# Two-layer hybrid decoder trunk: norm weights spread by one-column products, rank sums in one pass, the experts' order ahead of the gates, the first expert unit in halves

## The chip, the cores and the metric

The kernel runs on one NeuronCore of a Trainium2 chip. The metric is the device time of one execution in microseconds (us).

## The reference

The input is x, 256 tokens of 1024 channels, float32. Two layers run one after the other. Each has a mixer part (three groups of heads that read one RMS-normed input: a convolution, an SSD scan and latent attention, with one output projection behind them) and a channel mixer. In layer 1 the channel mixer sends each token to two of eight experts:

```
h = h + concatenate([y_conv, y_ssd, y_mla]) @ w_out[i]
hn = rms_norm(h, ffn_norm_g[i])                 # the norm weights g_ffn of the text
logits = hn @ router                            # 256 x 8
top_val, top_idx = top_k(logits, 2)
gates = softmax(top_val)
y[token] += gate * ((silu(hn @ wg[e]) * (hn @ wu[e])) @ wd[e])   # for both experts e of a token
h = h + y;  h = h + (p[i] @ ple_w_proj[i]) * sigmoid(rms_norm(h, g) @ ple_w_gate[i])
```

Each expert has three matrices of 1024 x 3584 (wd 3584 x 1024). Layer 0 has one dense SwiGLU in place of the experts. A last RMS norm ends the trunk.

## The kernel before

Nothing schedules the kernel but its own text: each engine's program is written out by hand, in `block.tensor`, `block.scalar`, `block.vector`, `block.sync` and `block.gpsimd`, and engines wait for each other on semaphores. Each engine works through its list in order.

**Weights.** All large weights come in units of 128 partitions x 2048 float32 (1 MB). SyncE issues the transfers into `ring`, which has 7 slots (`SLOTS`); unit g goes to slot g mod 7, once TensorE has read the unit seven before it. A unit is then parted in two, so that products can be made in fp32r: ScalarE copies it to `w_hi` (`split`, L1354, in the expert part `moe_split`, L1360), six of which exist, and VectorE writes what is left to `ring_lo` (L1856, L1862). TensorE waits for `lo_ready` of the unit and makes three products for each tile: high by high, high by low, low by high (`product`, L556 to L558).

**Mixers' end, layer 1.** VectorE adds up the scan's parts and multiplies them with the gate z (L2106, `ygz_ready`). ScalarE squares the result (L1531), takes roots (L1535) and squares the conv part (L1537, `csq`); VectorE makes reciprocals (L2121), scales, and writes the rests of the transposed heads (L1868, L1869). TensorE transposes (L814), makes the variance of the conv part (L823) and then runs four output units, pair 3 first, into four PSUM banks. VectorE adds the sums to h (L2154) and writes xs = h * g_ffn (L2158), for which the 1024 norm weights must stand in every partition, in `gain_of`. They lie one to a partition at the start. The kernel makes them so: ScalarE scales the identity by each of eight columns (`gain_diag_f`, L1522), TensorE multiplies by a square of ones (L804), and ScalarE copies out of PSUM (L1526).

**Routing.** TensorE makes the logits (L942). VectorE takes the two largest of each token (L2195 to L2219) and writes 0/1 rows, `counted`. TensorE sums them in three float32 products (L947 to L949): by a triangle for a token's rank within its expert, by ones for the experts' counts. VectorE makes the gates from ScalarE's exponential (L1615, L2224 to L2229), puts them with the ranks, the experts' numbers and the counts in a `table` of six vectors of eight, and sorts all six by count (L2245 to L2253). From the sorted table come the number of pairs and the experts' order (`order`, L2256 to L2262, `flag_ready`), then the slots of the tokens and the first selection matrix (`build_sel`, L2280).

**Experts.** SyncE waits for `flag_ready`, loads an expert's number into a register and issues its units (28 units of wg and wu, 14 of wd; 336 in all for eight experts). An expert pair has a heavy one (up to 128 tokens a step) and a light one (64). TensorE gathers tokens by products with the selection matrix (`gather`, L964); ScalarE and VectorE take them out as high part and rest, first half of the channels ahead of unit 0 and second half behind unit 1 (`take_heavy`). Unit c of the heavy expert (`in_unit`) has 12 products of 512 columns. On ScalarE and VectorE the parting runs four units ahead (`MOE_LEAD`), with the gate's silu (L1637) in ScalarE's list ahead of unit 7.

## Time and profile before

| | |
|---|---|
| median of 3 runs | 1526.2 us (1523.24 to 1528.65) |
| profiled execution, its own time | 1526.69 us |
| its span, first to last instruction | 1524.9 us |
| TensorE busy | 1458.8 us (96%) |
| VectorE busy | 1211.4 us (79%) |
| ScalarE busy | 1025.2 us (67%) |
| HBM traffic | 289 GB/s over the span |

The span is from one profiled execution; what lies around it is 1.8 us. Matmuls are pipelined: a row's length is longer than the distance to the next, and the distance is what a product costs. A float32 product leaves two records, an fp32r product one.

### The profile page before, as it was taken

The page shows a single profiled execution, that of the slowest core. Times are in us where ns is not written, and L with a number is a line of the kernel's source. Part 1 is how long each engine was busy: PE and PEld are TensorE (multiplying, and loading weights), DVE is VectorE, ACT ScalarE, POOL GpSimd, SP SyncE. Part 2 cuts the span into 40 slices and gives each one's busy share as a digit, 9 for nine tenths or more (in the row PEclk, how much of TensorE's full clock was granted, in tenths as well). Part 3 has the DMA queues.
Part 4 walks back from the last instruction along what each step waited for, and adds up shares of the span by engine and source line. Part 5 has one row for each costly group of instructions (what it writes and reads, how often), then busy time and mean ns, then how long its engine had stood idle before and what let it go on. Part 6 is the DMA issues. An engine that isn't in the chain of part 4 may idle for free.

```text
span 1524.9 us, 18697 instructions
## 1 busy us (share of the span) xinstructions
PE 1458.8 (96%) x7062; PEld 1199.6 (79%) x7062; DVE 1211.4 (79%) x1122; ACT 1025.2 (67%) x960; POOL 5.6 (0%) x12
## 2 busy tenths in 40 slices
PE   6989999999899879999999999999999999999997
PEld 5867888888797668878888887887877887887766
DVE  4996544653579769899999999999889999889973
ACT  5565443441655648778878788877788877788854
POOL 0000000000000000000000000000000000000000
PEclk9999999999999989999999999999999999999999
DMA  9414555555440049999999999999999999999980
GB/s 301 155 67 145 185 190 194 180 185 193 151 159 36 0 165 409 344 393 409 399 387 405 363 410 408 390 398 381 352 410 407 383 398 379 347 410 406 369 300 28
DMA packets 143865, 441.83 MB, mean 290 GB/s; under 512 B 6928, under 2 KB 21552, under 8 KB 143776
## 3 DMA queue, kind: packets, MB, share of 16 engines
q1 hardware_dynamic: 143104, 438.51, 76.8%
q0 software_dynamic: 672, 2.13, 0.4%
q8 instruction: 57, 0.93, 0.2%
q14 instruction: 32, 0.26, 0.0%
HBM read 439.56 MB, written 1.05 MB: 289 GB/s over the span
## 4 chain that ended last, share of the span: by engine, by line
PE 80%; DMA 9%; DVE 6%; ACT 3%; issue 1%; SPq 0%; DVEq 0%; ACTq 0%
PE psum L556 17%; PE psum L558 17%; PE psum L557 17%; DMA ring<-in_moe_w_down 5%; PE psum L1022 4%; PE psum L1023 4%; PE psum L1045 3%; PE psum L1046 3%; PE psum L1075 3%; PE psum L604 3%; DMA ring<-in_moe_w_up 3%; DVE ring_lo L1862 2%; PE psum L971 2%; PE psum L964 2%; ACT w_hi L1360 2%; PE psum L577 1%
## 5 line engine op out<-in xcount | busy, mean ns | idle before, releaser
L1862 DVE TENSOR_TENSOR ring_lo<-ring,w_hi 128x2048 fp32r<-128x2048 f32 x337 | 764.8, 2288 | 82.0 <-ACT w_hi L1360 79.5
L1360 ACT ACTIVATE w_hi<-ring 128x2048 fp32r<-128x2048 f32 x337 | 643.0, 1917 | 147.0 <-DMA ring<-in_moe_w_up 53.6
L1856 DVE TENSOR_TENSOR ring_lo<-ring,w_hi 128x2048 fp32r<-128x2048 f32 (+1 forms) x69 | 155.0, 2266 | 112.4 <-ACT w_hi L1354 112.4
L558 PE MATMUL psum<-w_hi,hidden_b 128*128 128x512 f32 x560 | 219.3, 392 | 0.0
L556 PE MATMUL psum<-w_hi,hidden_b 128*128 128x512 f32 x448 | 180.0, 402 | 3.7 <-DVE ring_lo L1856 3.7
L1022 PE MATMUL psum<-w_hi,xT_parts 128*128 128x512 f32 x448 | 180.0, 402 | 1.0 <-DVE ring_lo L1862 0.7
L557 PE MATMUL psum<-ring_lo,hidden_b 128*128 128x512 f32 x448 | 175.1, 391 | 0.0
L1023 PE MATMUL psum<-ring_lo,xT_parts 128*128 128x512 f32 x448 | 174.9, 391 | 0.0
L556 PE MATMUL psum<-w_hi,xT_parts 128*128 128x512 f32 (+1 forms) x384 | 149.7, 390 | 5.0 <-DVE xT_parts L1869 3.0
L1354 ACT ACTIVATE w_hi<-ring 128x2048 fp32r<-128x2048 f32 (+1 forms) x69 | 128.3, 1896 | 32.3 <-PE psum L558 27.8
L556 PE MATMUL psum<-w_hi,hidden_a 128*128 128x512 f32 x352 | 141.6, 402 | 8.6 <-DVE ring_lo L1862 8.4
L558 PE MATMUL psum<-w_hi,xT_parts 128*128 128x512 f32 (+1 forms) x384 | 148.9, 388 | 0.0
L557 PE MATMUL psum<-ring_lo,xT_parts 128*128 128x512 f32 (+1 forms) x384 | 148.8, 388 | 0.0
L557 PE MATMUL psum<-ring_lo,hidden_a 128*128 128x512 f32 x352 | 137.2, 390 | 0.0
L558 PEld LDWEIGHTS psum<-w_hi,hidden_b 128*128 128x128 f32 x560 | 105.4, 188 | 22.6
L556 PEld LDWEIGHTS psum<-w_hi,hidden_b 128*128 128x128 f32 x448 | 84.6, 189 | 22.2 <-DVE ring_lo L1856 3.9
L1022 PEld LDWEIGHTS psum<-w_hi,xT_parts 128*128 128x128 f32 x448 | 84.2, 188 | 22.3 <-DVE ring_lo L1862 5.8
L557 PEld LDWEIGHTS psum<-ring_lo,hidden_b 128*128 128x128 f32 x448 | 84.7, 189 | 18.5 <-issue 1.4
L1023 PEld LDWEIGHTS psum<-ring_lo,xT_parts 128*128 128x128 f32 x448 | 84.2, 188 | 16.0
L558 PE MATMUL psum<-w_hi,hidden_a 128*128 128x512 f32 x240 | 93.9, 391 | 0.0
L556 PEld LDWEIGHTS psum<-w_hi,hidden_a 128*128 128x128 f32 x352 | 66.1, 188 | 30.8 <-DVE ring_lo L1862 18.3
L556 PEld LDWEIGHTS psum<-w_hi,xT_parts 128*128 128x128 f32 x384 | 72.5, 189 | 19.3 <-DVE ring_lo L1856 5.1
(329 smaller groups left out, 1871.2 us busy)
## 6 DMA issues: line engine op xcount, KB each, us to landing
ring<-in_moe_w_gate SPq DMA_DIRECT2D x112, 1024.0 KB, 8.8
ring<-in_moe_w_up SPq DMA_DIRECT2D x112, 1024.0 KB, 8.9
ring<-in_moe_w_down SPq DMA_DIRECT2D x112, 1024.0 KB, 8.6
ring<-in_w_in SPq DMA_DIRECT2D x16, 1024.0 KB, 5.2
ring<-in_dense_w_gate SPq DMA_DIRECT2D x14, 1024.0 KB, 5.0
ring<-in_dense_w_up SPq DMA_DIRECT2D x14, 1024.0 KB, 5.1
ring<-in_dense_w_down SPq DMA_DIRECT2D x14, 1024.0 KB, 4.9
ring<-in_w_out SPq DMA_DIRECT2D x8, 1024.0 KB, 4.8
```

Of the source, the lines that this page charges most:

```text
L556: mm(o, a[0], b[0], start=first, stop=False)
L557: mm(o, a[0], b[1], start=False, stop=False)
L558: return mm(o, a[1], b[0], start=False, stop=final)
L604: last = mm(o[:, m * SEQ:m * SEQ + SEQ], w[:, kt, m * P:m * P + P], xT[kt], start=kt == 0, stop=kt == KT - 1)
L1022: mm(o, xl_both[kt], w[0][:, q, cols], start=kt == 0, stop=False)
L1023: last = mm(o, xl_both[kt], w[1][:, q, cols], start=False, stop=kt == KT - 1)
L1045: mm(o, elT_both[kt], w[0][:, q, cols], start=kt == 0, stop=False)
L1046: last = mm(o, elT_both[kt], w[1][:, q, cols], start=False, stop=kt == FKT - 1)
L1354: A(high(g, sizes[g]), raw(g, sizes[g]), ACT.Copy).then_inc(hi_ready, 1)
L1360: A(high(g, in_moe=True), raw(g), ACT.Copy).then_inc(hi_ready, 1)
L1856: V.tensor_tensor(low(g, sizes[g]), raw(g, sizes[g]), f32(high(g, sizes[g])), ALU.subtract).then_inc(lo_ready, 1)
L1862: V.tensor_tensor(low(g), raw(g), f32(high(g, in_moe=True)), ALU.subtract).then_inc(lo_ready, 1)
```

## The change

Four edits. (1) `gain_of` is made without `gain_diag_f`: TensorE takes one column of norm weights, repeated 128 times, as the stationary side and the identity as the moving side, four products of 128 columns for each half. The second half is made behind the variance, in bank 4, and the output's second quarter moves to bank 0. ScalarE's eight copies go, and its two copies out of PSUM move behind the conv part. (2) `counted`, the triangle and a column of ones are held as fp32r, so that the rank sums are fp32r products; VectorE fills them. (3) The sort is a function of a part of the table. The experts' numbers are sorted first and `order` is written at once, then ranks, slots and selection, then counts and the number of pairs (`flag_ready` counts to 2), then gates. TensorE, ScalarE and VectorE wait for 2; SyncE waits for 1, and for 2 only ahead of its loop. (4) The first expert unit is parted in two halves of 1024 columns, and TensorE starts its first half on `first_lo`.

```diff
+                def gain_rows(half, b):
+
+                    o = banks.fill(pe, ("gain", half), b)
+                    for q in range(4):
+                        last = mm(o[:, q * P:q * P + P], lp(L, "g_ffn", 4 * half + q).to_broadcast([P, P]), ident,
+                                  start=True, stop=True)
+                    last.then_inc(banks.is_full(("gain", half)), 1)
+
                 if L == DEPTH - 1:
-                    pe.wait_ge(gain_diag, 1)
-                    for half, b in enumerate((3, 1)):
-                        o = banks.fill(pe, ("gain", half), b)
-                        mm(o, ones, gain_diag_f[:, half * 512:half * 512 + 512], start=True, stop=True).then_inc(
-                            banks.is_full(("gain", half)), 1)
+                    gain_rows(0, 3)
 
                 def y_transposed(j, b):
...
                 mm(o, group, csq.rearrange("p m s -> p (m s)"), start=True, stop=True).then_inc(
                     banks.is_full(("var", L)), 1)
+                if L == DEPTH - 1:
+                    gain_rows(1, 4)
                 for j in range(2):
...
                         t, half = divmod(n, 2)
                         if i == 0:
-                            acc[key] = banks.fill(pe, key, (7, 4, 5, 6)[n])
+                            acc[key] = banks.fill(pe, key, (7, 0, 5, 6)[n])
...
             pe.wait_ge(chosen_ready, 1)
             o = banks.fill(pe, ("rank",), 6)
-            mm(o[:, 0:3 * NE], tri, counted[:, 0:3 * NE], start=True, stop=False)
-            mm(o[:, 0:3 * NE], ones, counted[:, 5 * NE:], start=False, stop=False)
-            mm(o[:, 0:3 * NE], ones, counted[:, 2 * NE:5 * NE], start=False, stop=True).then_inc(
+            every = tri_r[:, P:].to_broadcast([P, P])
+            mm(o[:, 0:3 * NE], tri_r[:, 0:P], counted[:, 0:3 * NE], start=True, stop=False)
+            mm(o[:, 0:3 * NE], every, counted[:, 5 * NE:], start=False, stop=False)
+            mm(o[:, 0:3 * NE], every, counted[:, 2 * NE:5 * NE], start=False, stop=True).then_inc(
                 banks.is_full(("rank",)), 1)
 
...
-            def moe_unit(ready, g, kts):
-                pe.wait_ge(lo_ready, ready + 1)
+            def moe_unit(ready, g, kts, wait=True):
+                if wait:
+                    pe.wait_ge(lo_ready, ready + 1)
                 return tuple(b.rearrange("p (k n) -> p k n", k=kts) for b in (high(g, in_moe=True), low(g)))
...
                 u, r = divmod(c - 8 * ch, units)
-                w = moe_unit(unit_of(i, k, c), ring_of(k, c, is_start(i, k, c)), kts)
+                in_halves = is_start(i, k, c) and c == 0
+                w = moe_unit(unit_of(i, k, c), ring_of(k, c, is_start(i, k, c)), kts, not in_halves)
...
                     pe.wait_ge((g_free, u_free)[u], ch_done(i, k, ch) - 1)
                 for q in range(kts):
+                    if in_halves:
+                        pe.wait_ge(*((first_lo, 1), (lo_ready, S0 + 1))[q])
                     for half in range(halves):
                         kt = kts * r + q
...
                 pair(i)
+            sp.wait_ge(flag_ready, 2)
             last_pair = sp.value_load(order[0:1, 0:1], min_val=PAIRS - 1, max_val=2 * PAIRS - 1)
...
                 o = banks.filled(act, ("st", L))
                 A(st, o, ACT.Copy).then_inc(banks.is_free(("st", L)), 1)
 
-                if L == DEPTH - 1:
-                    for kt in range(KT):
-                        last = A(gain_diag_f[:, kt * P:kt * P + P], ident, ACT.Copy, scale=lp(L, "g_ffn", kt))
-                    last.then_inc(gain_diag, 1)
-                    for half in range(2):
-                        o = banks.filled(act, ("gain", half))
-                        A(gain_of[half], o, ACT.Copy).then_inc(banks.is_free(("gain", half)), 1)
                 warm_up()
                 act.wait_ge(ygz_ready, L + 1)
...
                 act.wait_ge(conv_hi_ready, 2 * L + 1)
                 A(yT_hi[:, 0:2, :], csq, ACT.Copy).then_inc(conv_hi_ready, 1)
+                if L == DEPTH - 1:
+                    for half in range(2):
+                        o = banks.filled(act, ("gain", half))
+                        A(gain_of[half], o, ACT.Copy).then_inc(banks.is_free(("gain", half)), 1)
...
-                    split(N0)
+                    act.wait_ge(loaded[N0 % SLOTS], landed(N0))
+                    act.wait_ge(*last_reader[PARTED[turn(N0) - HIGHS]])
+                    A(high(N0)[:, 0:CHUNK], raw(N0)[:, 0:CHUNK], ACT.Copy).then_inc(first_hi, 1)
+                    A(high(N0)[:, CHUNK:], raw(N0)[:, CHUNK:], ACT.Copy).then_inc(hi_ready, 1)
...
-                V.memset(counted, 0.0)
+                V.tensor_scalar(counted, iota[:, 0:8 * NE], 0.0, None, ALU.mult)
+                V.tensor_copy(tri_r[:, 0:P], tri)
+                V.tensor_copy(tri_r[:, P:], ones[:, 0:1])
...
-                V.tensor_tensor(chosen, o1, o2, ALU.add)
+                V.tensor_tensor(chosen_r, o1, o2, ALU.add)
                 V.tensor_tensor(counted[:, 4 * NE:5 * NE], o1[:, NE:], o2[:, NE:], ALU.add)
...
-                dve.wait_ge(ev_ready, 1)
-                step(V.tensor_scalar(g1, ev, 1.0, None, ALU.add))
-                step(V.reciprocal(g1, g1))
-                step(V.tensor_tensor(g2, ev, g1, ALU.mult))
-                V.tensor_tensor(pairs(o1), pairs(o1), each(g1), ALU.mult)
-                step(V.tensor_tensor(pairs(o2), pairs(o2), each(g2), ALU.mult))
-                V.tensor_tensor(table[:, 2:4, :], pairs(o1), pairs(o2), ALU.add)
-                V.tensor_copy(table[:, 4, :], iota[:, 0:NE])
-
+                V.tensor_copy(table[:, 2, :], iota[:, 0:NE])
...
 
+                def across(v, n):
+                    return v.unsqueeze(1).to_broadcast([P, n, NE])
+
+                def sort(v0, n):
+
+                    rows = slice(v0, v0 + n)
+                    step(V.tensor_tensor(picked[:, rows], where.unsqueeze(1).to_broadcast([P, n, NE, NE]),
+                                         table[:, rows].unsqueeze(2).to_broadcast([P, n, NE, NE]), ALU.mult))
+                    step(V.tensor_reduce(ranked[:, rows], picked[:, rows], AX.X, ALU.add))
 
                 dve.wait_ge(chosen_ready, 1)
                 o = banks.filled(dve, ("rank",))
-                V.tensor_tensor(table[:, 0:2, :], pairs(o[:, 0:NT * NE]), pairs(chosen), ALU.mult)
-                V.tensor_copy(table[:, 5, :], o[:, 2 * NE:3 * NE]).then_inc(banks.is_free(("rank",)), 1)
-                dve.wait_ge(*banks.taken(("rank",)))
-
...
-                step(V.scalar_tensor_tensor(out=key, in0=table[:, 5, :], scalar=float(NE), in1=iota[:, 0:NE],
+                step(V.scalar_tensor_tensor(out=key, in0=o[:, 2 * NE:3 * NE], scalar=float(NE), in1=iota[:, 0:NE],
                                             op0=ALU.mult, op1=ALU.subtract))
                 step(V.tensor_tensor(above, across(key, NE), key.unsqueeze(2).to_broadcast([P, NE, NE]), ALU.is_gt))
                 step(V.tensor_reduce(place, above, AX.X, ALU.add))
                 step(V.tensor_tensor(where, across(place, NE),
                                      iota[:, 0:NE].unsqueeze(2).to_broadcast([P, NE, NE]), ALU.is_equal))
-                step(V.tensor_tensor(picked, where.unsqueeze(1).to_broadcast([P, 6, NE, NE]),
-                                     table.unsqueeze(2).to_broadcast([P, 6, NE, NE]), ALU.mult))
-                step(V.tensor_reduce(ranked, picked, AX.X, ALU.add))
-
-
-                step(V.scalar_tensor_tensor(out=mx, in0=ranked[:, 5, 0:1], scalar=float(LIGHT - P),
-                                            in1=ranked[:, 5, PAIRS:PAIRS + 1], op0=ALU.add, op1=ALU.max))
-                step(V.tensor_scalar(mx, mx, LIGHT + 0.5, float(PAIRS), ALU.is_gt, ALU.mult))
-                V.tensor_scalar(order[:, 0:1], mx, float(PAIRS - 1), None, ALU.add)
-                ids = ranked[:, 4, :].rearrange("p (k i) -> p i k", k=2)
+                sort(2, 1)
+                ids = ranked[:, 2, :].rearrange("p (k i) -> p i k", k=2)
                 for b in range(2):
                     last = V.tensor_copy(order[:, 1 + b * NE:1 + b * NE + NE].rearrange("p (i k) -> p i k", k=2), ids)
                 last.then_inc(flag_ready, 1)
+
+                V.tensor_tensor(table[:, 0:2, :], pairs(o[:, 0:NT * NE]), pairs(chosen), ALU.mult)
+                V.tensor_copy(table[:, 3, :], o[:, 2 * NE:3 * NE]).then_inc(banks.is_free(("rank",)), 1)
+                dve.wait_ge(*banks.taken(("rank",)))
+                sort(0, 2)
 
                 def by_step(t, b, buf):
                     return buf[:, t, b * NE:b * NE + NE].rearrange("p (i k) -> p i k", k=2)
...
+                sort(3, 1)
+                step(V.scalar_tensor_tensor(out=mx, in0=ranked[:, 3, 0:1], scalar=float(LIGHT - P),
+                                            in1=ranked[:, 3, PAIRS:PAIRS + 1], op0=ALU.add, op1=ALU.max))
+                step(V.tensor_scalar(mx, mx, LIGHT + 0.5, float(PAIRS), ALU.is_gt, ALU.mult))
+                V.tensor_scalar(order[:, 0:1], mx, float(PAIRS - 1), None, ALU.add).then_inc(flag_ready, 1)
+
+                dve.wait_ge(ev_ready, 1)
+                step(V.tensor_scalar(g1, ev, 1.0, None, ALU.add))
+                step(V.reciprocal(g1, g1))
+                step(V.tensor_tensor(g2, ev, g1, ALU.mult))
+                V.tensor_tensor(pairs(o1), pairs(o1), each(g1), ALU.mult)
...
-                split(N0)
+                dve.wait_ge(first_hi, 1)
+                V.tensor_tensor(low(N0)[:, 0:CHUNK], raw(N0)[:, 0:CHUNK], f32(high(N0)[:, 0:CHUNK]),
+                                ALU.subtract).then_inc(first_lo, 1)
+                dve.wait_ge(hi_ready, S0 + 1)
+                V.tensor_tensor(low(N0)[:, CHUNK:], raw(N0)[:, CHUNK:], f32(high(N0)[:, CHUNK:]),
+                                ALU.subtract).then_inc(lo_ready, 1)
                 split(N0 + 1)
```

ScalarE's list, between the copies of the mixers' scores and the squares, in the kernel before (`small` is `gain_of`, `arena_a<-par` the scaled identities, `xs` the gated product; the table load is that of the root):

```order
L1516 ACTIVATE arena_b<-psum 128x512 x3
L1518 ACTIVATE arena_b<-psum 128x512
L1522 ACTIVATE arena_a<-par 128x128 x8
L1526 ACTIVATE small<-psum 128x512 x2
L1367 ACT_TABLE_LOAD
L1367 ACTIVATE tiny<-par 128x1
L1531 ACTIVATE arena_b,tiny<-xs 128x256 x4
L1535 ACTIVATE tiny<-tiny 128x4
```

and in the changed kernel (L1538 are the squares):

```order
L1530 ACTIVATE arena_b<-psum 128x512 x3
L1532 ACTIVATE arena_b<-psum 128x512
L1381 ACT_TABLE_LOAD
L1381 ACTIVATE tiny<-par 128x1
L1538 ACTIVATE arena_b,tiny<-xs 128x256 x4
L1542 ACTIVATE tiny<-tiny 128x4
```

Ten copies have left the place; the table load follows the last score copy. Further on, ScalarE's list before has the parting of two output units around the conv part's silu:

```order
L1354 ACTIVATE w_hi<-ring 128x2048
L1557 ACT_TABLE_LOAD
L1557 ACTIVATE arena_a<-arena_a,par 128x256 x2
L1560 ACTIVATE xT_parts<-arena_a 128x512
L1354 ACTIVATE w_hi<-ring 128x2048
```

and the changed one:

```order
L1368 ACTIVATE w_hi<-ring 128x2048
L1564 ACT_TABLE_LOAD
L1564 ACTIVATE arena_a<-arena_a,par 128x256 x2
L1567 ACTIVATE xT_parts<-arena_a 128x512
L1571 ACTIVATE small<-psum 128x512 x2
L1368 ACTIVATE w_hi<-ring 128x2048
```

The two copies to `small` stand there between the conv part and the parting of the last output unit.

VectorE's list in the routing before, from the ranks to the casts into `order` (`route` is the table, `arena_b` holds key, order matrix and sorted vectors):

```order
L2237 TENSOR_TENSOR route<-psum,tiny 128x16
L2238 COPY route<-psum 128x8
L2245 SCALAR_TENSOR_TENSOR arena_b<-route,par 128x8
L2247 TENSOR_TENSOR arena_b<-arena_b 128x64
L2248 TENSOR_REDUCE arena_b<-arena_b 128x8
L2249 TENSOR_TENSOR arena_b<-arena_b,par 128x64
L2251 TENSOR_TENSOR arena_b<-arena_b,route 128x384
L2253 TENSOR_REDUCE arena_b<-arena_b 128x48
L2256 SCALAR_TENSOR_TENSOR tiny<-arena_b 128x1
L2258 TENSOR_SCALAR tiny<-tiny 128x1
L2259 TENSOR_SCALAR order<-tiny 128x1
L2262 CAST order<-arena_b 128x8 x2
```

and in the changed kernel, from the experts' numbers to the same casts and the first three steps behind them:

```order
L2239 COPY route<-par 128x8
L2240 TENSOR_TENSOR arena_b<-par 128x64
L2254 SCALAR_TENSOR_TENSOR arena_b<-psum,par 128x8
L2256 TENSOR_TENSOR arena_b<-arena_b 128x64
L2257 TENSOR_REDUCE arena_b<-arena_b 128x8
L2258 TENSOR_TENSOR arena_b<-arena_b,par 128x64
L2248 TENSOR_TENSOR arena_b<-arena_b,route 128x64
L2250 TENSOR_REDUCE arena_b<-arena_b 128x8
L2263 CAST order<-arena_b 128x8 x2
L2266 TENSOR_TENSOR route<-psum,counted 128x16
L2267 COPY route<-psum 128x8
L2248 TENSOR_TENSOR arena_b<-arena_b,route 128x128
```

The gates (L2224 to L2229, not shown) and the three steps to `order`'s pair count have left the way to the casts, and the sort before them is of 64 elements, not 384.

## Rows read from the trace of the kernel before

**Rows 1.** Windows, TensorE: us, busy (records), clock, DMA share, GB/s
```profile
600.00:640.00 40.00, 40.00 (x190) 1.00 1.02 390
```

**Rows 2.** Time line of ScalarE, mixers' end: start, us, line, tiles, [idle before <-releaser]
```profile
501.17 2.45 ACT L1522 ACTIVATE arena_a<-par 128x128 f32<-128x128 f32 x8
508.36 0.60 ACT L1526 ACTIVATE small<-psum 128x512 f32<-128x512 f32 x1 [4.73 <-PE psum L804]
...
511.24 0.40 ACT L1531 ACTIVATE arena_b<-xs 128x256 f32<-128x256 f32 x1
```

**Rows 3.** Time line of VectorE, mixers' end
```profile
506.16 1.22 DVE L2106 TENSOR_TENSOR xs<-xs,arena_a 128x1024 f32<-128x1024 f32 x1
...
513.29 0.18 DVE L2121 RECIPROCAL tiny<-tiny 128x4 f32<-128x4 f32 x1 [4.41 <-ACT tiny L1535]
...
516.76 0.75 DVE L1868 TENSOR_TENSOR xT_parts<-psum,xT_parts 128x256 fp32r<-128x256 f32 x2
...
529.95 2.29 DVE L1856 TENSOR_TENSOR ring_lo<-ring,w_hi 128x2048 fp32r<-128x2048 f32 x1 [1.11 <-ACT w_hi L1354]
```

**Rows 4.** Time line of TensorE, mixers' end
```profile
507.25 1.94 PE L804 MATMUL psum<-arena_a,par 128*128 128x512 f32 x4
...
517.61 0.47 PE L556 MATMUL psum<-w_hi,xT_parts 128*128 128x512 f32 x1 [0.28 <-issue]
```

**Rows 5.** Time line of TensorE, one-column products of layer 1
```profile
486.33 3.74 PE L740 MATMUL psum<-par,tiny 128*128 128x128 f32 x32
```

**Rows 6.** Time line of TensorE, output's end, rank sums and first gather
```profile
539.50 3.73 PE L577 MATMUL psum<-par,h 128*128 128x128 f32 x32
...
548.48 0.62 PE L947 MATMUL psum<-tiny,par 128*128 128x24 f32 x2 [1.77 <-DVE tiny L2219]
...
549.35 0.60 PE L949 MATMUL psum<-tiny,par 128*128 128x24 f32 x2
554.90 5.31 PE L964 MATMUL psum<-arena_b,xs 128*128 128x128 f32 x30 [4.95 <-DVE arena_b L2280]
```

**Rows 7.** Time line of VectorE, routing
```profile
549.55 0.17 DVE L2224 TENSOR_SCALAR tiny<-tiny 128x2 f32<-128x2 f32 x1 [1.13 <-ACT tiny L1615]
...
551.02 0.17 DVE L2245 SCALAR_TENSOR_TENSOR arena_b<-route,par 128x8 f32<-128x8 f32 x1
...
552.00 0.56 DVE L2251 TENSOR_TENSOR arena_b<-arena_b,route 128x384 f32<-128x384 f32 x1
...
553.63 0.23 DVE L2262 CAST order<-arena_b 128x8 int32<-128x8 f32 x2
...
554.05 0.60 DVE L2280 TENSOR_SCALAR arena_b<-par,tiny 128x128 f32<-128x128 f32 x2
...
559.32 0.69 DVE L1868 TENSOR_TENSOR hidden_b<-psum,hidden_b 128x512 fp32r<-128x512 f32 x1 [4.09 <-ACT hidden_b L1623]
```

**Rows 8.** Time line of SyncE's queue, first expert transfers
```profile
554.86 2.32 SPq L1261 DMA_DIRECT2D ring<-in_moe_w_gate  x4
```

**Rows 9.** Time line of ScalarE, first expert units
```profile
558.69 0.60 ACT L1623 ACTIVATE hidden_b<-psum 128x512 fp32r<-128x512 f32 x1 [9.17 <-PE psum L964]
559.84 1.91 ACT L1354 ACTIVATE w_hi<-ring 128x2048 fp32r<-128x2048 f32 x1 [0.55 <-DMA ring<-in_moe_w_gate]
562.40 1.91 ACT L1354 ACTIVATE w_hi<-ring 128x2048 fp32r<-128x2048 f32 x1 [0.65 <-DMA ring<-in_moe_w_gate]
```

**Rows 10.** Time line of TensorE, first product of expert units 0 and 1
```profile
564.13 0.50 PE L556 MATMUL psum<-w_hi,hidden_b 128*128 128x512 f32 x1 [3.69 <-DVE ring_lo L1856]
...
568.40 0.57 PE L556 MATMUL psum<-w_hi,hidden_b 128*128 128x512 f32 x1
```

**Rows 11.** Time line of ScalarE, its first gate
```profile
578.43 1.03 ACT L1637 ACTIVATE arena_b<-psum 128x1024 f32<-128x1024 f32 x1
```

**Rows 12.** Time line of VectorE, expert unit 7
```profile
581.29 2.29 DVE L1862 TENSOR_TENSOR ring_lo<-ring,w_hi 128x2048 fp32r<-128x2048 f32 x1 [1.85 <-ACT w_hi L1360]
```

**Rows 13.** Windows: busy of PE, PEld, DVE, ACT, POOL; clock, DMA share, GB/s
```profile
566.00:567.00 1.00, 1.00 (x4) 0.81 (x3) 1.00 (x2) 0.88 (x1) 0.00 (x0) 0.50 1.03 410
```

27 lines of the change are left out of this document (15 added, 12 removed).

## The prediction

> **What bounds the kernel now.** I began with the stretches of the expert part, since it fills two thirds of the span. From 600 to 640 us TensorE is busy 40.00 of 40 us at full clock, while the transfers of that core move 390 GB/s [rows 1]. In such a stretch TensorE sets the pace, and the ring of weight units follows it through the slots that it frees. So a microsecond gained or lost ahead of it, and not eaten by a wait for a weight unit on the way, should stand at the end. The question is then what sets the time at which TensorE gets there. I read the time lines of the two places that the change touches.
>
> The first is the end of layer 1's mixers. VectorE writes the last gated product at 506.16, 1.22 us long, so it is there at 507.38 [rows 3]. ScalarE needs it for four squares, yet its first square starts at 511.24 [rows 2]: it stood in its queue behind the copies of the norm weights, which waited for TensorE's two 512-column products (507.25, 1.94 us for four records) [rows 4] and then behind the table load that the root wants. VectorE's reciprocal (513.29) had sat idle 4.41 us for what ScalarE makes of the squares [rows 3]. Its split and its rest of the transposed heads follow, and then TensorE's first output product at 517.61 [rows 4]. The reader is to see a chain here: squares, root, reciprocal, scaling, split, rest, product, with nothing in it that waits for the norm weights.
>
> The second is the routing. VectorE waits 1.13 us for ScalarE's exponential (549.55), works out the gates, and takes up the ranks only at 551.02; the order of experts is written at 553.63 + 0.23 = 553.86 [rows 7]. SyncE's first expert transfer is issued at 554.86 [rows 8]; ScalarE takes the unit up at 559.84, VectorE ends its rest 4.2 us later, and TensorE starts at 564.13 after 3.69 us of idleness [rows 9, 10]. Transfers, not the gathered tokens, are late there: ScalarE sat 0.55 us for the transfer after it had taken the first half of the tokens (558.69, 0.60 us) [rows 9].
>
> **Norm weights.** ScalarE loses eight copies (2.45 us) [rows 2]. They lay in its wait for 507.38, so I price them at nothing; the cover is the 4.73 us that ScalarE stood idle behind them, and no more than 2.45 us could come of them. The two copies out of PSUM (0.60 us each) move behind the conv part, so that the table load and its one-element root run ahead of 507.38, in that idle time. The squares then start about 507.4 in place of 511.24: **3.8 us**, for the rest of the chain moves as one. On TensorE two 512-column products of 1.94 us become eight one-column products; the nearest row has sixteen of the same kind (32 records) in 3.74 us, 0.23 each [rows 5], so 1.9 us against 1.94, half of it now between the variance and the last transposes. TensorE waits there anyhow: the conv square that its variance product wants comes about 510.0, the variance takes half of 1.94, the four products 0.9, the eight transposes 0.9, which ends at 512.8. VectorE's rest, which releases the output products, ended at 516.76 + 0.75 = 517.5 [rows 3] and now ends at 513.7, so TensorE's start moves with it.
>
> What can be late next is the last output unit. VectorE's rest of it ends at 529.95 + 2.29 = 532.24 [rows 3]. TensorE does 96 products from 517.61 to 539.50 [rows 4, 6], 0.228 each, and comes to the last 24 at 534.0: 1.8 us of room. The two copies put 1.2 us ahead of this split on ScalarE. About 0.6 us of room stays, so nothing is lost; without it each microsecond would count in full. The bank change (second quarter of the output in bank 0) asks TensorE to wait for VectorE's second sum before its first transpose. That sum is taken before TensorE ends its last product; nothing.
>
> **Rank sums.** The new fills (a product of 64 columns, a copy of 128) stand in VectorE's wait for the logits; nothing. Six records from 548.48 to 549.95, the pairs 0.435 us apart, some 0.22 us from record to record [rows 6]; three records should end about 549.2, and VectorE's key can start at 549.3. The bounds are 548.9 (the sums nearly free) and 550.0 (one pass as long as two). I take 549.3, since both kinds of record load the same 128 columns. The page "FP8 and Floating Point Precision" of the Trainium skill (TensorE Precision Notes) counts four passes for true FP32; the records show two per product. By the page's ratio the sums would end near 548.9, and the sum below would gain 0.4 us more.
>
> **Numbers ahead of gates.** From the key to the sort takes 0.98 us (551.02 to 552.00) in four steps [rows 7]; it stays. The sort of six vectors (two steps, the first 0.56 us long) and the three steps for the pair count took 1.63 us, to 553.63; in their place come two steps over 64 elements, about 0.26 each, and the same casts of 0.23. So the order is there at 549.3 + 0.98 + 0.52 + 0.23 = 551.03, **2.8 us** earlier, and so is each transfer: SyncE waits for the first count of the flag alone.
>
> The selection is behind it: two route copies, a sort of two vectors (0.6 us; two steps over 128 elements, each between 0.26 for 64 and 0.56 for 384), the slots, and the 0.60 us of rows 7. It ends near 552.7, and the gather starts at 552.95 in place of 554.90 [rows 6]. The first half of tokens is out at 556.75 and taken at 557.35; unit 0 lands at 557.0. The gather is thus late by 0.35 us, not the transfer. Pair count and gates come after the selection: about 3.4 us of VectorE's small steps until 556.1, and then its register load; what waits behind them is the rest of the tokens, at 557.4. In the kernel before this place held 4.09 us of idleness [rows 7], which is the cover. TensorE, ScalarE and VectorE wait for the second count at 553.8, well ahead.
>
> **First unit in halves.** A half costs ScalarE about 1.03 us (the 128x1024 row) and VectorE half of 2.29, 1.15 [rows 11, 12]. TensorE starts at 557.35 + 1.03 + 1.15 = 559.6. But unit 1 is taken up by ScalarE at 562.40 - 2.83 = 559.57 and is ready after 1.92 and 2.29 us, at 563.85; TensorE idles some 1.4 us before it. Before, it began unit 1 at 568.40, because it had started late and ran at half clock in between (0.50 from 566 to 567) [rows 10, 13]. That is 4.55 us earlier at full clock. Without the halves TensorE would start unit 0 at 561.6 and unit 1 at 564.4: they are worth 0.55 us, and only for the moment, for at unit 7 the split stands behind ScalarE's first gate. It was ready at 581.29 + 2.29 = 583.58 [rows 12] and moves with the transfers to 580.75; TensorE, which came to it at 568.40 + 72 x 0.228 = 584.8, now comes at 580.25. It waits 0.5 us. The second place gives 4.55 - 0.5 = **4.05 us**.
>
> **The sum.** 3.8 + 4.05 = 7.85 us. The profiled execution took 1526.69 us (span 1524.9), so 1518.8; the median of the three runs, 1526.2, lies 0.5 us lower, within their spread. What a measurement can tell from no change is about 0.3%, 4.6 us.
>
> **Rivals.**
> A: the clock falls in the first units after all. TensorE still idles 3.7 us ahead of the gather, 1.1 us before unit 0 and 1.4 us before unit 1. Before, the half clock took unit 0 from some 2.7 to 4.27 us [rows 10], 1.5 us. Once in the new schedule ahead of unit 7, it brings TensorE there at 581.75 or later, and the second place gives some 2.8 us: 1520.1. The page "TensorE: Matmul & The Clock Gate" (Why this matters for your kernels) warns of idle gaps between bursts, because the clock falls back to half. This trace agrees: half clock after the idleness of 560.4 to 564.1. By that rule A is likelier than my sum; but the idle pieces are now shorter than those that a fall followed.
> B: one of the two places gives nothing: the conv part's split late by 4 us, or the gather or the gates holding unit 0 and 1 until 568. Then 1522.6 to 1522.9, no change that can be told. Against it stands the room of 0.6 us and 1.2 us worked out above; for it, that both rooms are short.
> C: slower. The expert stream is 336 units at 2.56 us (562.40 less 559.84) [rows 9], 860 us; TensorE now stands nearer to it. Should the units come at an interval longer by 1.5%, in the stretches where they set the pace, that costs 12.9 us against 7.85: 1531.7. It decides from 0.9% on. Nothing in the change touches the issue of a transfer behind the first, so little speaks for it.
> D: the rank sums in one pass take as long as two (key at 550.0): 0.7 us less from the second place, 1519.5. It lies inside the forecast.
>
> **How the numbers follow.** Forecast with D 0.57, A 0.21, B 0.16, C 0.06. The likeliest is 1518.8, its own range 1516.5 to 1520.5 with the spread of the runs. To hold 8 in 10 the range goes up into B, to 1522.8, and down to 1515.5 (0.4 us for the sums, and 2.7 us that the runs shown spread about their median). Faster by over 0.3% is below 1521.6: forecast and A and a little of B, 0.80. Within 0.3%: 0.15. Slower: 0.05.
>
> **What would show it.** Right: ScalarE's first square 0.1 us behind VectorE's gated product; the first output product near 513.8; the interval from the end of the logits to the first expert transfer shorter by 2.8 us; from there to unit 1's first product 11.8 us in place of 13.5; the last unit of the mixers not waited for; span near 1517.0. Wrong: a wait of TensorE for the last output unit; the gates running into the rest of the tokens; half clock between unit 0 and unit 7; or a stretch at full transfer rate with more idle TensorE than before, which would give part of the gain back later.

## The result, and the profile after

| kernel | median, us | runs | lowest and highest | profiled span |
|---|---|---|---|---|
| before | 1526.01 | 14 | 1521.51 to 1529.34 | 1524.9 |
| changed | 1517.45 | 14 | 1515.37 to 1523.0 | 1516.2 |

The ratio is 0.9947, 95% interval 0.9935 to 0.996: 8.1 us less, between 6.1 and 9.9. The forecast of 1518.8 was 7.85 us less. The profiled execution of the changed kernel itself took 1518.02 us. Of the kernels tried below, early_silu had one execution at about half the usual rate, its profiled one (2965.67 us): it is left out below, and early_look is another execution of the same kernel.

The spans differ by 8.7 us, and not all of it is the change's. Below are the first TensorE record of the changed kernel and the gated product that ends the mixers.

```profile
13.29 4.93 PE L579 MATMUL psum<-xs,h 128*128 128x128 f32 x23 [13.29 <-DVE xs L1862]
...
504.68 1.22 DVE L2120 TENSOR_TENSOR xs<-xs,arena_a 128x1024 f32<-128x1024 f32 x1
```

The gated product of before started at 506.16 [rows 3], and its first TensorE record at 14.76: some 1.48 us were there before any changed instruction ran. They come with the first inputs: ScalarE's first square waits for the parameters' transfer until 9.54 before and until 8.08 in the changed kernel. So from here on I compare intervals and not absolute times.

**First place.** ScalarE, the mixers' end, in the changed kernel:

```profile
505.93 0.42 ACT L1538 ACTIVATE arena_b<-xs 128x256 f32<-128x256 f32 x1 [4.59 <-DVE xs L2120]
...
522.42 1.06 ACT L1571 ACTIVATE small<-psum 128x512 f32<-128x512 f32 x2
523.37 1.92 ACT L1368 ACTIVATE w_hi<-ring 128x2048 fp32r<-128x2048 f32 x1
```

VectorE there, the reciprocal and the rest of the last output unit; and TensorE's first output product, one product 72 behind it, and the output's end:

```profile
508.00 0.18 DVE L2135 RECIPROCAL tiny<-tiny 128x4 f32<-128x4 f32 x1 [0.60 <-ACT tiny L1542]
...
525.32 2.29 DVE L1870 TENSOR_TENSOR ring_lo<-ring,w_hi 128x2048 fp32r<-128x2048 f32 x1 [2.09 <-ACT w_hi L1368]
```

```profile
512.33 0.47 PE L558 MATMUL psum<-w_hi,xT_parts 128*128 128x512 f32 x1 [0.89 <-DVE ring_lo L1870]
...
528.77 0.39 PE L558 MATMUL psum<-w_hi,xT_parts 128*128 128x512 f32 x1
...
534.21 3.73 PE L579 MATMUL psum<-par,h 128*128 128x128 f32 x32
```

The gated product is there at 504.68 + 1.22 = 505.90 and the square starts at 505.93. Before, that gap was 511.24 - 507.38 = 3.86 us [rows 2, 3]. The reciprocal's wait for ScalarE fell from 4.41 us to 0.60. The two copies (1.06 us for both) now stand ahead of the last output unit's split. Its rest ends at 527.61, and TensorE comes to it at 528.77 without a wait: 1.16 us of room, where 0.6 was forecast.

**Second place.** TensorE, from the rank sums to the first products of units 0 and 1:

```profile
543.19 0.28 PE L956 MATMUL psum<-counted,tri_parts 128*128 128x24 f32 x1 [1.77 <-DVE counted L2235]
543.32 0.31 PE L957 MATMUL psum<-counted,tri_parts 128*128 128x24 f32 x1
543.48 0.37 PE L958 MATMUL psum<-counted,tri_parts 128*128 128x24 f32 x1
547.66 6.65 PE L973 MATMUL psum<-arena_b,xs 128*128 128x128 f32 x32 [3.81 <-DVE arena_b L2286]
554.39 0.47 PE L558 MATMUL psum<-w_hi,hidden_b 128*128 128x512 f32 x1
...
558.70 0.50 PE L558 MATMUL psum<-w_hi,hidden_b 128*128 128x512 f32 x1 [1.35 <-DVE ring_lo L1870]
```

VectorE from the key to the halves:

```profile
543.96 0.17 DVE L2254 SCALAR_TENSOR_TENSOR arena_b<-psum,par 128x8 f32<-128x8 f32 x1 [0.62 <-PE psum L958]
...
545.45 0.25 DVE L2263 CAST order<-arena_b 128x8 int32<-128x8 f32 x2
...
550.46 0.23 DVE L2370 COPY tiny<-arena_b 128x8 f32<-128x8 f32 x2
552.07 0.69 DVE L1882 TENSOR_TENSOR hidden_b<-psum,hidden_b 128x512 fp32r<-128x512 f32 x1 [1.38 <-ACT hidden_b L1634]
553.02 1.22 DVE L2376 TENSOR_TENSOR ring_lo<-ring,w_hi 128x1024 fp32r<-128x1024 f32 x1 [0.25 <-ACT w_hi L1696]
```

The key starts 0.77 us behind the first rank product (forecast 549.3 - 548.48 = 0.82), the order 1.49 us behind the key (1.50 forecast). The gates end at 550.69; the rest of the tokens had to wait for ScalarE until 552.07, so 1.38 us of cover was left (1.2 to 1.3 forecast). SyncE's queue, then the granted clock (windows of TensorE alone: stretch, us, busy, clock, DMA share, GB/s):

```profile
546.69 2.44 SPq L1274 DMA_DIRECT2D ring<-in_moe_w_gate  x4
```

```profile
542.00:543.00 1.00, 0.00 (x0) 1.00 0.00 0
543.00:544.00 1.00, 0.66 (x3) 0.69 0.00 0
545.00:552.00 7.00, 4.34 (x20) 0.50 0.61 208
553.00:554.00 1.00, 1.00 (x8) 0.69 1.02 418
555.00:566.00 11.00, 9.65 (x43) 1.00 1.03 410
```

After the idleness behind the logits nearly the whole gather runs at half clock (6.65 us): the granted clock rises between 553 and 554, and unit 0 starts at 554.39. The time lines give the same milestones in each kernel, below. The first column counts from the end of the gated product, the second is the output's 96 products, the others count from the output's end (in the changed kernel 534.21).

| us | first output product | 96 products | first expert transfer | gather | unit 0 | unit 1 | unit 7 |
|---|---|---|---|---|---|---|---|
| before | 10.23 | 21.89 | 15.36 | 15.40 | 24.63 | 28.90 | 45.42 |
| changed | 6.43 | 21.88 | 12.48 | 13.45 | 20.18 | 24.49 | 41.43 |
| gain_only | 6.42 | 21.88 | 15.36 | 15.41 | 24.79 | 28.91 | 45.63 |
| route_only | 10.22 | 21.87 | 12.63 | 13.60 | 20.33 | 24.53 | 41.47 |
| diag_late | 6.42 | 21.85 | 12.59 | 13.56 | 20.29 | 24.54 | 41.48 |
| more_copies | 6.43 | 24.20 | 12.63 | 13.60 | 20.33 | 24.60 | 41.54 |
| whole_unit | 6.42 | 21.85 | 13.70 | 14.67 | 23.24 | 27.55 | 43.88 |
| whole_again | 6.43 | 21.88 | 12.60 | 13.57 | 22.13 | 26.59 | 42.94 |
| whole_fill | 6.41 | 21.88 | 13.05 | 14.02 | 22.43 | 25.28 | 43.24 |
| changed_again | 6.42 | 21.85 | 13.76 | 14.73 | 21.47 | 25.65 | 42.59 |
| f32_sums | 6.43 | 21.85 | 13.95 | 14.92 | 21.67 | 25.90 | 42.84 |
| early_look | 6.42 | 21.84 | 13.04 | 14.01 | 20.54 | 24.92 | 41.80 |
| by_max | 6.43 | 21.84 | 11.61 | 13.35 | 19.18 | 23.60 | 40.80 |

Where the first expert transfer comes later than 12.7 in a kernel whose routing is that of the changed one, the logits before it took longer; that is the last section's. The step from 12.48 to about 12.6 is the clock in the rank sums: VectorE's key stands 0.77 us behind the first of them in the changed kernel, where the clock falls only within them (0.69 from 543 to 544), and 0.93 us in route_only, where it is 0.50 throughout. Behind it the rows repeat closely, so I compare units with the transfer as zero.

### The profile page after: what moved, and what is told of

Read it like the earlier page. It is cut to its first block, busy times and chain, and to the rows that moved or that the text cites. A ratio compares the mean times of both kernels' runs of the same rounds, so it can differ in the third digit from the quotient of the medians.

```text
span 1516.2 us, 18716 instructions
## 1 busy us (share of the span) xinstructions
PE 1455.6 (96%) x7071; PEld 1199.0 (79%) x7071; DVE 1212.3 (80%) x1131; ACT 1022.6 (67%) x953; POOL 5.6 (0%) x12
## 4 chain that ended last, share of the span: by engine, by line
PE 80%; DMA 9%; DVE 6%; ACT 3%; issue 1%; SPq 0%; DVEq 0%; ACTq 0%
PE psum L558 17%; PE psum L560 17%; PE psum L559 17%; DMA ring<-in_moe_w_down 4%; PE psum L1035 4%; PE psum L1036 4%; PE psum L1058 3%; PE psum L1059 3%; DMA ring<-in_moe_w_up 3%; PE psum L1088 3%; PE psum L606 3%; PE psum L980 2%; DVE ring_lo L1876 2%; PE psum L973 2%; ACT w_hi L1374 2%; PE psum L579 1%
```

## The experiments

**One place at a time.** gain_only is the kernel before with the norm weights' part of the change; route_only is the changed kernel with the norm weights as before; diag_late keeps the eight scaled copies and the two 512-column products, and moves ScalarE's two copies behind the conv part as the change does.

```diff
 diag_late, against the changed kernel
-                        mm(o[:, q * P:q * P + P], lp(L, "g_ffn", 4 * half + q).to_broadcast([P, P]), ident,
-                                  start=True, stop=True)
+                    mm(o, ones, gain_diag_f[:, half * 512:half * 512 + 512], start=True, stop=True)
...
+                    for kt in range(KT):
+                        last = A(gain_diag_f[:, kt * P:kt * P + P], ident, ACT.Copy, scale=lp(L, "g_ffn", kt))
```

> The norm weights' part alone, on the kernel before. My theory (the squares wait behind the two copies, and all that follows moves as one): from the end of the gated product to the first output product 6.4 us in place of 10.2, the routing as before (28.9 us from the end of the output products to unit 1's first product), and 3.8 us less in all, a ratio of 0.9975. Rival (the two places are not additive, because the expert stream takes back what comes early): the interval is 6.4 us too, but the time falls by less than 2 us.

> All but the norm weights' part. My theory: 10.2 us at the mixers' end as before, first expert transfer 12.5 us behind the output products in place of 15.4, unit 1 at 24.5 in place of 28.9, and 4.0 us less in all, a ratio of 0.9974. Rival (the wait at unit 7 does not bind): up to 4.6 us. Rival (the stream takes it back): under 2 us.

> The changed kernel, with the norm weights made by eight scaled identities and two 512-column products again, but with the second product and the two copies left where the change puts them. My theory (only the place of the two copies counts): gated product to first output product 6.4 us, time as the changed kernel within 0.5 us. Rival (the eight copies or the wide products cost something): the interval is 7 us or more, up to 2.45 us longer.

Measured: gain_only 1521.27 us, ratio 0.9965 (0.9952 to 0.9979), which is 5.3 us; route_only 1522.86, 0.9977 (0.9963 to 0.9991), 3.5 us; diag_late 1518.49, 0.9947 (0.9931 to 0.9963). In the table each place moves its own interval alone: 3.81 us and 3.95 us at unit 7. The two add up to 8.8 us by the ratios, 7.8 by the intervals, 8.1 measured for both. diag_late has every interval of the changed kernel within 0.15 us: the one-column products are worth nothing by themselves. What counts is that the two copies, and with them the second product, which diag_late moves too, no longer stand ahead of the squares.

**The first unit whole.** whole_unit is the changed kernel without the halves. whole_again is another execution of the same kernel, beside changed_again, another one of the changed kernel. whole_fill puts nine fp32 products of 128 columns, whose results nobody reads, behind the gather.

```diff
 whole_unit, against the changed kernel
-                    if in_halves:
-                        pe.wait_ge(*((first_lo, 1), (lo_ready, S0 + 1))[q])
...
-                    A(high(N0)[:, 0:CHUNK], raw(N0)[:, 0:CHUNK], ACT.Copy).then_inc(first_hi, 1)
-                    A(high(N0)[:, CHUNK:], raw(N0)[:, CHUNK:], ACT.Copy).then_inc(hi_ready, 1)
+                    split(N0)
 whole_fill, further
+            for _ in range(9):
+                mm(psum[:, 7, 0:P], ident, tri, start=True, stop=True)
```

> The changed kernel, with the first expert unit parted whole. My theory: unit 0 starts 2.0 us later (some 22.2 us behind the output products in place of 20.2), unit 1 about 0.4 to 0.6 us later than 24.5, unit 7 as in the changed kernel, time the same within 0.5 us. Rival (the halves keep the clock up): without them half clock comes between unit 0 and unit 7, and 1.2 us or more are lost.

> The changed kernel with the first expert unit parted whole, and nine idle float32 products (2 us at full clock, into a PSUM bank that nobody reads) between the gather and unit 0. With the unit whole and no such products, TensorE idled 2.4 us, unit 0 ran at half clock, and unit 1 stood 13.85 us behind the first transfer, unit 7 at 30.2, against 12.0 and 28.9 with the halves. Theory (that loss is the clock's, and the halves are worth it because they end the idleness sooner): unit 0 at full clock, unit 1 at 12.6 and unit 7 at 28.9. Rival (half clock there has nothing to do with the idleness, it falls in some executions): half clock between unit 0 and 2 all the same, unit 7 at 30.

> A second look at the kernel with the first unit whole. Theory (the idleness ahead of unit 0 brings half clock): again half clock in unit 0 or 1, unit 7 some 30 us behind the first transfer. Rival (chance): full clock, unit 7 at 28.9 and only the start of unit 0 late.

> A second execution of the changed kernel under the profiler, to see how far two executions of one program agree. Theory (the mixers' end and the start of the experts repeat, the expert stream doesn't): 6.4 us, first transfer at 12.5 plus what half clock adds in the logits, unit 7 at 28.9 behind it; the rest of the span differs by up to 2 or 3 us. Rival: the whole span behind the routing repeats within 0.5 us.

Measured: my theory for whole_unit missed, and its rival came true. whole_unit 1520.54 us, ratio 0.9958 (0.9941 to 0.9975); the intervals of this ratio and of the changed kernel's overlap. whole_fill, one execution, 1519.37; whole_again 1515.58; changed_again 1517.38. These totals don't tell the halves apart, the stretches do. TensorE in whole_again at unit 0, and the granted clock there (all engines):

```profile
557.43 0.50 PE L558 MATMUL psum<-w_hi,hidden_b 128*128 128x512 f32 x1 [2.02 <-DVE ring_lo L1865]
...
558.42 0.63 PE L558 MATMUL psum<-w_hi,hidden_b 128*128 128x512 f32 x1
558.85 0.63 PE L559 MATMUL psum<-ring_lo,hidden_b 128*128 128x512 f32 x1
```

```profile
555.00:557.00 2.00, 0.41 (x4) 0.21 (x2) 1.92 (x1) 1.59 (x2) 0.00 (x0) 1.00 1.03 422
...
558.00:559.00 1.00, 1.00 (x4) 0.80 (x3) 1.00 (x1) 0.98 (x1) 0.00 (x0) 0.50 1.04 418
559.00:561.00 2.00, 2.00 (x7) 1.52 (x6) 2.00 (x3) 1.35 (x2) 0.00 (x0) 0.50 1.03 410
```

The same place in whole_unit:

```profile
559.02 0.79 PE L558 MATMUL psum<-w_hi,hidden_b 128*128 128x512 f32 x1 [2.43 <-DVE ring_lo L1865]
```

```profile
559.00:560.00 1.00, 0.98 (x2) 0.83 (x3) 1.00 (x1) 0.84 (x2) 0.00 (x0) 0.50 1.04 418
560.00:562.00 2.00, 2.00 (x6) 1.57 (x5) 2.00 (x3) 1.51 (x1) 0.00 (x0) 0.50 1.01 403
```

In both executions TensorE idles 2.0 and 2.4 us between the gather and the whole unit, and unit 0 then runs for six to eight products at half clock (0.43 us from product to product in place of 0.23). Counted from the first transfer, unit 1 starts after 13.85 and 13.99 us; in all eight executions that have halves it starts after 11.88 to 12.01. Unit 7 starts after 30.18 and 30.34 us against 28.95 and 28.83 in the changed kernel. So the halves are worth 1.8 to 2.1 us at unit 1, and 1.2 to 1.5 us of it is still there at unit 7.

Half clock is one part of that price, and the late start of the unit the other. With the filler products the clock stays full in a whole unit 0, which takes 2.85 us, and unit 1 starts after 12.23 us: the halves are then worth 0.2 to 0.3 us, less than the 0.55 of the forecast. The opposite case is by_max, below, which has halves and half clock: TensorE idles 2.02 us ahead of unit 0, most of its products take half clock, and it ends about when unit 1 is ready.

```profile
553.88 0.57 PE L558 MATMUL psum<-w_hi,hidden_b 128*128 128x512 f32 x1 [2.02 <-DVE ring_lo L2383]
554.25 0.63 PE L559 MATMUL psum<-ring_lo,hidden_b 128*128 128x512 f32 x1
554.67 0.63 PE L560 MATMUL psum<-w_hi,hidden_b 128*128 128x512 f32 x1
...
558.30 0.46 PE L558 MATMUL psum<-w_hi,hidden_b 128*128 128x512 f32 x1
```

The last line is unit 1's first product, 11.99 us behind by_max's first transfer (546.31) and without a wait. The four cases, in us from the first transfer to unit 1:

| unit 0 | full clock | half clock |
|---|---|---|
| in halves | 11.88 to 12.01 | 11.99 (by_max) |
| whole | 12.23 (whole_fill) | 13.85, 13.99 |

Either the early start or the full clock is enough; only a late start and half clock together cost more than 0.3 us. With halves unit 0 starts 7.5 to 7.7 us behind the transfer (whole: 9.4 to 9.5), and the 1.35 us that TensorE idles ahead of unit 1 in the changed kernel is what takes up the half clock in by_max. whole_fill and by_max are one execution each, and by_max differs in its routing too.

whole_fill's unit 7 can't be used: unit 6's transfer landed late (ScalarE waited 1.94 us for it), and the gate's table load, the gate and unit 7's parting stand behind it. changed_again starts unit 7 at 28.83 us behind its transfer, as its theory had it, but from there to the end of its span takes 937.3 us against 940.6 in the changed kernel: the rest differs by 3.3 us, and its rival falls.

**More copies in ScalarE's way.** more_copies puts three extra copies of 1024 columns, 3.23 us together, one after the other, ahead of the two of the norm weights.

```diff
+                    for n in range(3):
+                        A(dx.rearrange("p t c -> p (t c)"), par[:, 0:2 * SSDW], ACT.Copy).then_inc(extra, 1)
+                        act.wait_ge(extra, n + 1)
```

> The changed kernel with three more ScalarE copies of 1024 columns (about 1.05 us each, 3.2 us in all, into a buffer that nobody reads) ahead of the two copies of the norm weights, and so ahead of the parting of the last output unit. My theory (that split has 1.1 us of room in the changed kernel's trace, 0.6 in my forecast, and behind it each microsecond counts): TensorE waits about 2.1 us ahead of the last 24 output products, 96 products take 24.0 us in place of 21.9, and the time rises by 2.1 us. Rival (the room is larger, since VectorE stands idle 2.09 us ahead of that split): no wait, or under 1 us.

Measured: 1520.15 us, ratio 0.9967 (0.9952 to 0.9982). The last output unit in it, TensorE:

```profile
529.65 0.50 PE L558 MATMUL psum<-w_hi,xT_parts 128*128 128x512 f32 x1 [2.06 <-DVE ring_lo L1873]
```

The output takes 24.20 us in place of 21.88, and the routing behind it is unchanged. The room is real, and what goes beyond it counts in full: 3.23 - 1.16 leaves 2.1 us, the interval is 2.3 longer, and the ratios make it 3.1 us with intervals that overlap.

**The rank sums.** f32_sums is the changed kernel with the sums' operands fp32 again, in the same three products.

```diff
-            mm(o[:, 0:3 * NE], tri_r[:, 0:P], counted[:, 0:3 * NE], start=True, stop=False)
+            mm(o[:, 0:3 * NE], tri, counted[:, 0:3 * NE], start=True, stop=False)
```

> The changed kernel with the rank sums as float32 products again. My theory (two records per product in place of one, and nothing else): from the start of the sums to VectorE's key 1.5 us in place of 0.8, and the first expert transfer 0.7 us later, some 13.2 us behind the output products in place of 12.5. Rival (the sums are hidden by VectorE's own steps): the transfer at 12.5 as before.

Measured in one execution: 1521.63 us. TensorE's sums and VectorE's key in it:

```profile
547.20 0.62 PE L955 MATMUL psum<-counted,par 128*128 128x24 f32 x2 [1.77 <-DVE counted L2234]
...
548.07 0.60 PE L957 MATMUL psum<-counted,par 128*128 128x24 f32 x2
...
548.79 0.17 DVE L2253 SCALAR_TENSOR_TENSOR arena_b<-psum,par 128x8 f32<-128x8 f32 x1 [1.44 <-PE psum L957]
```

Two records per product, and the key 1.59 us behind the first of them; in the changed kernel three records, and 0.77 us, 0.82 less. Some 0.15 of that is clock: f32_sums has 0.50 throughout its sums, and fp32r sums at that clock have the key after 0.93 us (route_only, changed_again). One pass saves 0.66 us at equal clock. The first transfer is at 13.95, later than the 13.2 of the theory, because the logits took 0.66 us longer in this execution (4.30 against 3.64); without that it would be at 13.29, so of the 2.88 us by which the changed kernel issues it earlier, 2.07 come from the order ahead of the gates.

**The first gate's table.** early_silu lets ScalarE load the gate's table in its idle time before the gather, not at the first gate.

```diff
+                    A(warm, const("ones", 1), ACT.Silu)
```

> The changed kernel with one silu of a single element on ScalarE behind its exponential, so that the table of the first gate is loaded while ScalarE waits for the tokens. My theory (at unit 7 the split stands behind the gate's table load, and that took 0.4 to 0.5 us back): the gate starts 1.3 us or less earlier, unit 7's first product 41.0 us behind the output products in place of 41.4, and 0.4 us less in all, too little for the time to tell. Rival (unit 7 waits for its transfer, not for the table): 41.4 as before.

> A second look at the changed kernel with the early silu; expectation as before: unit 7 at 41.0 by my theory, at 41.4 by the rival.

Measured: 1518.07 us (median of six executions), ratio 0.9948 (0.9928 to 0.9968): nothing against the changed kernel's 0.9947. In early_look the first gate comes 22.20 us behind the first transfer, in the changed kernel 23.75, but unit 7 starts after 28.76 us against 28.95 and 28.83. The table load of 1.28 us is out of the path, and the path gives back 0.1 to 0.2 us of it. Unit 7 is held by its own transfer almost as long as by the gate: ScalarE waits 1.25 us for it.

**A version with all that the runs pointed to.** by_max lets VectorE's MAX8 sort the eight keys, turns them to numbers at once, loads the gate's table early, and fills TensorE's idle time between the sums and the gather with eight products that nobody reads.

```diff
+                step(V.max(out=by_key, in_=key))
...
+                V.tensor_scalar(order[:, 1:1 + NE], two, NE - 1, None, ALU.bitwise_and)
...
+                    A(warm, const("ones", 1), ACT.Silu)
...
+            for _ in range(8):
+                mm(psum[:, 7, 0:P], ident, tri, start=True, stop=True)
```

> A version beyond the changed kernel: the experts' order comes from one maximum over the eight keys (VectorE's instruction gives them sorted) and two integer steps, ahead of the order matrix; eight idle float32 products keep TensorE at work between rank sums and gather; the silu table is loaded early. My theory (the first transfer sets the time, and the tokens now wait as long as it does): order 0.9 us earlier, first expert transfer at 11.6 us behind the output products in place of 12.5, unit 1 at 23.6 in place of 24.5, unit 7 at 40.1 in place of 41.4, and 1.3 us less in all, a ratio of 0.994 to the kernel before, too near to the changed one for the time to tell. Rival (the gather comes too late for the earlier transfer): unit 1 at 24.2 or later.

Measured: 1516.65 us, ratio 0.9936 (0.9911 to 0.9961). VectorE's order, and the gather on TensorE:

```profile
544.46 0.17 DVE L2258 SCALAR_TENSOR_TENSOR arena_b<-psum,par 128x8 f32<-128x8 f32 x1 [0.63 <-PE psum L958]
544.66 0.17 DVE L2261 MAX8 arena_b<-arena_b 128x8 f32<-128x8 f32 x1
...
545.15 0.17 DVE L2266 TENSOR_SCALAR order<-order 128x8 int32<-128x8 int32 x1
```

```profile
548.05 3.81 PE L976 MATMUL psum<-arena_b,xs 128*128 128x128 f32 x32 [0.36 <-DVE arena_b L2293]
```

The order stands 0.86 us behind the key, in the changed kernel 1.74; the transfer is 0.87 us earlier; the gather takes 3.81 us and not 6.65, for it has the full clock. But it now ends at 551.86, 2.02 us ahead of unit 0, and half clock comes there (the lines are above), so the fillers moved it and did not remove it; at unit 1 it costs nothing. Unit 1 is 0.89 us earlier behind the output, at 23.60 as forecast. Unit 7 is only 0.63 earlier, at 40.80, and not at the forecast's 40.1: ScalarE waited 2.18 us for unit 6's transfer ahead of it. By the intervals by_max is ahead by some 0.6 us; the timing can't tell the two kernels apart.

## Why the prediction was right, step by step

- **The squares in 507.38's place, 3.8 us.** Shown: 3.80 us in the changed kernel, 3.81 in gain_only alone. That nothing of the 2.45 us of removed copies would come of itself is shown by diag_late. The copies' own 0.6 us each are the smaller part of the 3.86: after 507.38 it was 0.98 us until TensorE's first product let the first copy start (508.36), 1.48 for the two copies with the wait between them, and 1.40 for the table load and the root behind them (509.84 to 511.24), which could have run earlier.
- **The last output unit's room.** Forecast 0.6 us, measured 1.16 us. Behind the first output product the last unit's rest started after 529.95 - 517.61 = 12.34 us before [rows 3, 4] and after 525.32 - 512.33 = 12.99 now, so the copies cost it 0.65 us and not the 1.2 I put down: ScalarE took them in 0.95 us, and its work ahead of them stood 0.3 us earlier. more_copies shows the mechanism.
- **Rank sums.** The key at 549.3 by the forecast; 0.77 us behind the sums is 549.25 on the clock of before. Rival D (no gain from one pass) fell with f32_sums. The page "FP8 and Floating Point Precision" of the Trainium skill (TensorE Precision Notes), with its four passes, led to 548.9. Two records per fp32 product don't speak against the page: in products of 512 columns the trace agrees with it in time. From 488.41 to 495.28 the changed kernel runs eight fp32 products of that width (L624), 0.86 us each, against 0.23 for an fp32r product of the same width, 3.8 to one. What doesn't carry over is the ratio to narrow products: with 24 columns, at half clock, it is 0.44 us against 0.22 (f32_sums, changed_again), and the forecast's reason, that each record loads the same 128 columns, fits but has no run of its own.
- **The order 2.8 us earlier.** The first transfer moved by 2.88 us, the gather by 1.95 (forecast 554.90 - 552.95 = 1.95). The forecast had the tokens and not the transfer set unit 0, and so it is: ScalarE took the first half of them at 551.45 and the unit at 551.94, without a wait for its transfer.
- **Unit 0 and unit 1.** Unit 0 was forecast 20.1 us behind the output's end, measured 20.18; unit 1 4.55 us earlier, measured 4.41; unit 7 4.05, measured 3.99. The wait ahead of unit 7 was forecast at 0.5 us and is 0.26, which makes up for part of what unit 1 lacks.
- **The halves, mis-sized.** The term "worth 0.55 us, and only for the moment" was wrong: it took the full clock for granted without them. Measured, they are worth 1.8 to 2.1 us at unit 1 and 1.2 to 1.5 at unit 7. The forecast's sum doesn't rest on the term, since it was for the kernel with halves.
- **Rival A.** Half clock in unit 0 is what happens to the kernel without halves. In the changed kernel it didn't happen, and there I had the idleness wrong: I forecast 1.1 us before unit 0, but the gather ran at half clock, ended at 547.66 + 6.65 = 554.31, and unit 0 followed at 554.39. That this closed gap was needed is not shown: more_copies and early_look idle 1.11 and 1.35 us there and have no half clock in unit 0 either. And rival A had the price wrong. It put half clock in unit 0 down at 1.5 us, with TensorE late at unit 7; but the forecast itself had 1.4 us of idleness ahead of unit 1, which covers nearly all of it. by_max shows that: half clock in unit 0, and unit 1 as soon behind its transfer as without. So, for half clock in unit 0, the forecast was safer than its chances said.
- **Rivals B and C.** B fell with the table: both places gave all. C asked for an expert interval longer by 0.9% or more. From 555 to 1380 us TensorE waits 7.5 us for the units' rests, 15 times; before it was 7.3 us, 17 times:

```profile
PE psum L558 <- DVE ring_lo L1876: 7.5, 15, 1.0
PE psum L558 <- DVE ring_lo L1870: 1.4, 1, 1.4
```

**What stays open.** 7.8 us stand at unit 7 in one profile pair, 7.2 (8.7 less 1.48) at the end. From the output's end to the end of the span take 985.4 us before and 982.0 in the changed kernel, but diag_late needs 981.3, more_copies 981.3, route_only 979.4 and f32_sums 982.2, with the same stream of units and starts of unit 7 that differ by 1.4 us at most. From unit 7 to the end of the span the two executions of the changed kernel take 940.6 and 937.3 us, before and gain_only, which are alike from the routing on, 940.0 and 943.3, and all thirteen lie between 935.6 and 943.3. So a single execution's stream varies by several us, more than what is left to explain, and a single pair of spans proves nothing here; the gain at the end rests on the medians. In the pair shown the tail alone is 2.7 us worse: after the last gate TensorE waits 6.1 us and not 3.4 in front of its last piece.

```profile
PE psum L980 <- ACT xT L1690: 6.1, 1, 6.1
```

Which transfer of the tail comes late, and whether an earlier issue has a part in it, no run here isolates.

## What to carry to other kernels

Ask of each instruction on an in-order engine what stands behind it, not what it costs: two copies of 0.6 us that nobody needed soon, with what they waited for and the table load behind them, held up a chain by 3.8 us, and the cheaper way to make their input was worth nothing. Give a consumer the first thing that it needs (the order of the units) before the things it needs later (gates, counts), and check that what was delayed still lies under other work. Where a matrix engine restarts after idleness, price the pieces behind the idleness with the clock that they will really have, and ask what they can hide under: half a unit early was put down at 0.55 us and was worth 1.8 to 2.1, because a late start and half clock together outran the slack ahead of the next unit; either alone cost 0.3 us or less.

## What the runs showed of the hardware that was not expected

**The clock can fall within the logits.** The 32 records of 8 columns take 3.64 us in the changed kernel; in changed_again, the same kernel, they and the clock were:

```profile
539.14 4.76 PE L950 MATMUL psum<-rt,arena_a 128*128 128x8 f32 x32
```

```profile
540.00:541.00 1.00, 1.00 (x11) 1.00 0.00 0
541.00:542.00 1.00, 1.00 (x8) 0.71 0.00 0
542.00:543.00 1.00, 1.00 (x6) 0.50 0.00 0
```

TensorE had been busy without a gap for more than the output's 22 us, and yet the granted clock fell to half. The stretch took 3.64 us in eight profiled executions, before's among them, 4.05 in two, and 4.30, 4.70 and 4.76 in one each; its code is the same in all. So this is a cost of up to 1.1 us that an execution pays or not. The page "TensorE: Matmul & The Clock Gate" of the Trainium skill (Why this matters for your kernels) speaks of idle gaps between bursts; the rows here show none, only narrow products. A pause shorter than a record would not show in them, since the records overlap.

**Equal idleness, unequal clock.** In whole_unit and whole_again the clock was full in the stretch before and fell behind 2.43 and 2.02 us without work, in by_max behind 2.02 us. In more_copies TensorE idled 2.06 us ahead of the last output unit, and the clock stayed at 1.00 from 529 to 542. There it had run 72 products without a gap before, 16 us at full clock; in whole_unit and whole_again the gather before the gap had run mostly at half clock. By contrast 1.77 us behind the narrow products of the logits were followed by half clock in the rank sums (1.00 from 542 to 543, 0.50 from 545 on), and 1.35 us before unit 1 in the changed kernel by nothing (clock 1.00 from 555 to 566). So the length of the last pause alone doesn't decide it in these rows. What does, no run here isolates.
